# Decay steps of a gated linear attention scan moved and divided in a two-part transformer kernel

## The chip, the cores and the metric

The kernel runs on one core of one Trainium2 chip. The metric is the device time of one execution in microseconds (us), given as the median of several executions.

## What is computed

The reference is a stack of two blocks of two layers each, in fp32, on 256 tokens of width 1024. The change concerns the second block alone, which also carries 256 context tokens, so it works on 512 rows in layer 0 and, for most products, on 256 in layer 1. From the normalised rows h it makes, among others, keys and queries (4 heads of 128), values (4 heads of 256), two ranks of 16 for the decays, and the four inputs of a convolution branch. Its gated linear attention is:

```
la_f = log_sigmoid(r_f @ w_df + b_df) / 16      # and la_b for the backward scan
for each chunk (64 rows), state s (dk x dv per head):
    bcum  = cumsum(la)
    o     = (q * exp(bcum)) @ s  +  sum over s<=t of q k exp(bcum_t - bcum_s) v
    s_new = exp(b_last) * s + (k * exp(b_last - bcum))^T @ v
o_ctx, s_f, s_b = scans of the context (forward and backward), from zero
o_lat           = scans of the tokens, from s_f and s_b
```

In the last layer the context's outputs are not needed, only its end states. After the scan each head's rows are divided by their root mean square, and the result is gated, multiplied with a branch weight and summed with the two other branches.

## The kernel before, in words

**Weights.** Every weight is loaded by SyncE in units of 512 KB (`load`, L2812) into five RAW buffers, and split: ScalarE writes a high part in fp32r (`split`, L1523, its line in the profile L1529), VectorE the remainder (`split`, L2083, L2095). There are four pairs of split buffers (NS). A split into a buffer waits until TensorE has finished the unit that had it before. TensorE forms each product in three passes (high x high, low x high, high x low): `turned` (L1048 to L1050) for outputs with features along the partitions, `straight` (L1061 to L1063) for outputs with rows along them.

**Order of the work.** A class `Schedule` writes one list of steps, and each engine runs the steps of the list that concern it, strictly in the list's order. `get_w` appends the splits and loads that may go ahead; the split of unit u+3 stands in the list right ahead of the products of unit u. PSUM has eight banks; `take(ring, name)` gives the free bank of a ring that was let go longest ago, and `give` frees it in the list; at run time TensorE waits for the last reader of the bank's previous use (`bank`, L1014). LO4 are banks 0 to 3, HI4 4 to 7.

**The scan** (`gla`, L500 on) is a generator; each `next` appends some steps. The function `block2` calls it beside other work: once or more per unit of the values' products by the table KEYS, then beside the convolution branch (`branch_a`: 8 x 4 weight units, each appended as two halves) by `weave`. There each half unit adds RA (2.0 in layer 0, 1.25 in layer 1) to an account, and the scan goes on while the account is 1 or more; a `yield n` costs n, a plain `yield` 1. A scan handles the context (s = 1) first, then the tokens (s = 0). For each of them:

- `gdec` (TensorE L1269): eight products of the ranks RT with the decay weights WDEC into four banks. RT and WDEC are each made in a high part by ScalarE and a low part by VectorE in step `rank` (ScalarE L1710 and L1713, VectorE L2362 and L2366), after the raw decay weights WRAW have come by a DMA that ScalarE issues (`wdec`, L1705) behind the DMAs that store x (`spill2`, L1697).
- `gdec2` (VectorE L2380): 16 conversions of 128x256, eight taking the maximum with LOWEST into E4, eight the minimum into ET; ScalarE exponentiates E4 in two halves (L1745).
- `gln`: ScalarE takes two logarithms (L1752), VectorE combines them with ET (two of L2389), ScalarE exponentiates twice (L1757).
- `ginit`: the start values in GW; ScalarE copies the keys twice (L1766), VectorE multiplies the queries twice (L2405).
- the doubling: `gprod` (TensorE L1299, 16 products of 128 columns), `keep` (VectorE L2442, L2448) and `gwiden` (VectorE L2420, L2426, L2430; ScalarE L1778) over eight levels, IC apart in the account. Where the outputs aren't needed (layer 1, context), `gwiden` alone.
- for the context `gke` (keys turned, TensorE L1067, copied by ScalarE L1797), `gst` (end states, TensorE L1323, copied L1804).
- `gout` (outputs, L1339 to L1344, copied L1809), `gsq` (squares, ScalarE L1819), `gnorm` (VectorE's reciprocal root, then POOL L2752).

Before the change all of layer 0's scan lies beside the branch (KEYS is all 0), and layer 1's first decays, start values and widenings lie under the two groups of value units (`gv`, L1735 copies each group's four banks once its four units are done, L1738). The turned keys, the end states and layer 1's second decays lie beside the branch, whose first product is `ba_mm` (L1347). The convolution of the branch is `ba_x` (L1844, L2471 to L2479).

## Time and profile before

| what | value |
|---|---|
| median of 3 runs | 2110.48 us (2109.89 to 2114.09) |
| the profiled execution's own time | 2109.92 us |
| its span, first to last instruction | 2108.1 us |
| mean granted TensorE clock | 0.992 |
| TensorE busy | 2064.2 us, 98% |
| VectorE busy | 1355.6 us, 64% |
| ScalarE busy | 955.8 us, 45% |

The time of a run is that of the device, the span that of the profiled execution's instructions. Busy times count overlapping matmuls once, and a matmul's recorded length is longer than the distance to the next one. Times inside the trace count from the start of the span. The second block runs from about 690 us on, its layer 0 scan beside the branch from 788 to 1040, its layer 1 from about 1594, with the scan up to 1815.

### The profile page before, as it was taken

The numbers are of one execution on the slowest core, as the hardware profiler recorded it, in microseconds if no ns is written. First come the engines' busy times: TensorE is split into PE (matmuls) and PEld (weight loads), VectorE is DVE, ScalarE is ACT, GpSimd is POOL, SyncE is SP. The second block draws the span as 40 slices with busy tenths as digits, with TensorE's granted clock in tenths as the row PEclk, the third lists the DMA queues.
The fourth block names the chain that finished last, engine by engine and source line by source line (L and its number), as shares of the span: only waits on it lengthen the run. The fifth ranks groups of instructions, "written<-read, shape, count | busy, mean of one in ns | idle before, by whom it ended". The sixth has DMA issues, their size and how long they took to land.

```text
span 2108.1 us, 31387 instructions
## 1 busy us (share of the span) xinstructions
PE 2064.2 (98%) x12082; PEld 1781.1 (84%) x12082; DVE 1355.6 (64%) x2381; ACT 955.8 (45%) x1568; POOL 135.7 (6%) x140
## 2 busy tenths in 40 slices
PE   9999999999999999999999999999999989999998
PEld 6779998778999888888888778888888889888997
DVE  6757667667777328568445555868555588575665
ACT  5555555555555424353323453232244554445443
POOL 1001000000110100000200001111110000100100
PEclk9999999999999999999999999999999999999999
DMA  9437656525555422222222104534234334251553
GB/s 255 139 131 253 224 208 210 168 93 170 181 180 180 140 96 65 70 70 70 80 90 90 60 21 161 185 117 155 95 119 153 103 125 144 91 180 54 194 172 131
DMA packets 79731, 285.79 MB, mean 136 GB/s; under 512 B 8976, under 2 KB 9628, under 8 KB 79584
## 3 DMA queue, kind: packets, MB, share of 16 engines
q1 hardware_dynamic: 71136, 256.93, 36.4%
q10 hardware_dynamic: 6416, 19.51, 2.6%
q0 software_dynamic: 2032, 7.35, 1.4%
q8 instruction: 97, 1.59, 0.3%
q14 instruction: 50, 0.41, 0.1%
HBM read 277.92 MB, written 5.83 MB: 135 GB/s over the span
## 4 chain that ended last, share of the span: by engine, by line
PE 82%; DVE 9%; ACT 5%; issue 2%; POOL 0%; DVEq 0%; ACTq 0%
PE pb L1048 16%; PE pb L1050 16%; PE pb L1049 16%; PE pb L1061 6%; PE pb L1063 6%; PE pb L1062 6%; DVE SPL L2095 3%; PE pb L1067 2%; PE pb L1227 2%; PE pb L1228 2%; PE pb L1229 2%; PE pb L1299 2%; ACT SPH L1529 2%; PE pb L1402 2%; PE pb L1383 2%
## 5 line engine op out<-in xcount | busy, mean ns | idle before, releaser
L2095 DVE TENSOR_TENSOR SPL<-RAW,SPH 128x1024 fp32r<-128x1024 f32 x460 | 560.1, 1232 | 395.4 <-ACT SPH L1529 371.4
L1048 PE MATMUL pb<-HTH,SPH 128*128 128x256 f32 (+1 forms) x2008 | 645.9, 322 | 10.6 <-DVE SPL L2095 6.2
L1050 PE MATMUL pb<-HTH,SPL 128*128 128x256 f32 (+1 forms) x2008 | 637.8, 318 | 0.0
L1049 PE MATMUL pb<-HTL,SPH 128*128 128x256 f32 (+1 forms) x2008 | 637.6, 318 | 0.0
L1529 ACT ACTIVATE SPH<-RAW 128x1024 fp32r<-128x1024 f32 x462 | 478.3, 1051 | 238.9 <-PE pb L1050 117.7
L1048 PEld LDWEIGHTS pb<-HTH,SPH 128*128 128x128 f32 x2008 | 382.9, 191 | 39.5 <-issue 7.3
L1049 PEld LDWEIGHTS pb<-HTL,SPH 128*128 128x128 f32 x2008 | 383.0, 191 | 26.4
L1050 PEld LDWEIGHTS pb<-HTH,SPL 128*128 128x128 f32 x2008 | 382.7, 191 | 26.0
L1061 PE MATMUL pb<-SPH,HTH 128*128 128x512 f32 x640 | 255.0, 398 | 0.5 <-DVE QNB L2536 0.5
L1063 PE MATMUL pb<-SPL,HTH 128*128 128x512 f32 x640 | 250.3, 391 | 0.0
L1062 PE MATMUL pb<-SPH,HTL 128*128 128x512 f32 x640 | 250.3, 391 | 0.0
L1061 PEld LDWEIGHTS pb<-SPH,HTH 128*128 128x128 f32 x640 | 121.2, 189 | 27.2 <-issue 2.6
L1063 PEld LDWEIGHTS pb<-SPL,HTH 128*128 128x128 f32 x640 | 120.7, 189 | 26.0
L1062 PEld LDWEIGHTS pb<-SPH,HTL 128*128 128x128 f32 x640 | 121.0, 189 | 23.7
L1048 PE MATMUL pb<-ABH,SPH 128*128 128x512 f32 (+1 forms) x384 | 130.7, 340 | 1.7 <-DVE SPL L2095 0.9
L1049 PE MATMUL pb<-ABL,SPH 128*128 128x512 f32 (+1 forms) x384 | 128.9, 336 | 0.0
L1050 PE MATMUL pb<-ABH,SPL 128*128 128x512 f32 (+1 forms) x384 | 128.8, 335 | 0.0
L1896 ACT ACTIVATE GT<-pb,BG 128x512 f32<-128x512 f32 (+1 forms) x48 | 27.8, 579 | 118.5 <-PE pb L1050 118.5
L1048 PEld LDWEIGHTS pb<-ABH,SPH 128*128 128x128 f32 x384 | 72.1, 188 | 11.0 <-issue 2.2
L1050 PEld LDWEIGHTS pb<-ABH,SPL 128*128 128x128 f32 x384 | 72.0, 187 | 8.9
L1049 PEld LDWEIGHTS pb<-ABL,SPH 128*128 128x128 f32 x384 | 72.1, 188 | 8.6 <-issue 0.2
L1227 PE MATMUL pb<-SPH,AH 128*128 128x512 f32 x176 | 71.6, 407 | 2.2 <-ACT SPH L1529 1.8
(284 smaller groups left out, 2489.4 us busy)
## 6 DMA issues: line engine op xcount, KB each, us to landing
RAW<-in_w_up SPq DMA_DIRECT2D x88, 512.0 KB, 4.5
RAW<-in_wa SPq DMA_DIRECT2D x64, 512.0 KB, 3.3
RAW<-in_w_in SPq DMA_DIRECT2D x48, 512.0 KB, 5.1
RAW<-in_wmg SPq DMA_DIRECT2D x48, 512.0 KB, 3.3
RAW<-in_wbr SPq DMA_DIRECT2D x48, 512.0 KB, 3.3
RAW<-in_w_down SPq DMA_DIRECT2D x44, 512.0 KB, 4.7
RAW<-in_w_ada SPq DMA_DIRECT2D x24, 512.0 KB, 4.6
ARAW<-in_w_ada ACTq DMA_DIRECT2D x24, 512.0 KB, 4.3
```

The source lines that it names most:

```text
L1048: T.matmul(o, wh[:, kt, :], xh[:, kt, n0:n1], start=kt == 0, stop=False)
L1049: T.matmul(o, wh[:, kt, :], xl[:, kt, n0:n1], start=False, stop=False)
L1050: m = T.matmul(o, wl[:, kt, :], xh[:, kt, n0:n1], start=False, stop=kt == 7)
L1061: T.matmul(P[:, :], xh[:, kt, c], wh[:, j, :], start=kt == 0, stop=False)
L1062: T.matmul(P[:, :], xl[:, kt, c], wh[:, j, :], start=False, stop=False)
L1063: m = T.matmul(P[:, :], xh[:, kt, c], wl[:, j, :], start=False, stop=kt == 7)
L1067: return T.transpose(o, i, ident)
L1227: T.matmul(P[:, :], xh, wh, start=j == 0, stop=False)
L1228: T.matmul(P[:, :], xl, wh, start=False, stop=False)
L1229: m = T.matmul(P[:, :], xh, wl, start=False, stop=end)
L1529: A.activation(hi, raw, ACT.Copy, scale=1.0).then_inc(*act.tick(s["hi"], ("u", u)))
L2095: W.tensor_tensor(lo, raw, hi.bitcast(F32), SUB).then_inc(*dve.tick(s["lo_dve"], ("u", u)))
```

## The change

It divides the decays into three steps, `gdec2` (maximum conversions and first exponentials), `gln` (minimum conversions, logarithms, combination) and a new `gexp` (second exponentials), with other work between them by GAPS. E4 moves within the memory that GW, KE and XS share, so that it lies over two parts of GW that the turned keys KE don't use. The scan is written anew as a sequence: first decays, start values, doubling, keys turned, (layer 0: end states, outputs), second decays, (layer 1: end states), start values, (layer 0: norm of the first scan's rows), doubling, outputs, norm. In layer 0 the first decays and start values go under the second group of value units, which takes banks 4 to 7. In layer 1 one `next` of the scan follows each of the four key units, and KEYS gives 1, 2, 2, 2 and 2, 3, 1, 2 for the eight value units. IC, PC and the waits follow.

```diff
--- before.py
+++ after.py
@@ -33,8 +33,9 @@
 LO4, HI4, LOW6, LOW7, ALL8 = (0, 1, 2, 3), (4, 5, 6, 7), (0, 1, 2, 3, 4, 5), (0, 1, 2, 3, 4, 5, 6), (0, 1, 2, 3, 4, 5, 6, 7)
 
 RA = [2.0, 1.25]
-IC, PC = (4, 5), (8, 17)
-KEYS = ((0,) * 8, (2, 1, 1, 2, 2, 2, 2, 1))
+IC, PC = (4, 6), (3, 1)
+GAPS = ((1, 2), (2, 3))
+KEYS = ((0, 0, 0, 0, 1, 1, 1, 2), (1, 2, 2, 2, 2, 3, 1, 2))
 LOWEST = -30.0
 EARLY = 3
 FIRST = 11
@@ -555,66 +556,96 @@
             self.give(n)
             yield
 
+    def decays(self, l, s, ring):
+        self.add("mark", f"gla{l}{s}")
+        for i in range(4):
+            self.take(ring, ("gd", l, s, i))
+            self.add("gdec", l, s, i)
+        yield
+        self.add("gdec2", l, s)
+        yield GAPS[l][0]
+        self.add("gln", l, s)
+        for i in range(4):
+            self.give(("gd", l, s, i))
+        yield GAPS[l][1]
+        self.add("gexp", l, s)
+        yield
+
+    def doubling(self, l, s, ring):
+        full = gla_full(s, l)
+        if full:
+            for hp in range(2):
+                self.take(ring, ("gp", l, s, -1, hp))
+            self.add("gprod", l, s, -1)
+            yield LEAD[l][s]
+        for j in range(SPANS + full):
+            if full and j < SPANS:
+                for hp in range(2):
+                    self.take(ring, ("gp", l, s, j, hp))
+            if full:
+                self.add("keep", l, s, j - 1)
+                for hp in range(2):
+                    self.give(("gp", l, s, j - 1, hp))
+            if j < SPANS:
+                if full:
+                    self.add("gprod", l, s, j)
+                self.add("gwiden", l, s, j)
+            yield IC[l] if full else 1
+
+    def keys_turned(self, l, ring):
+        for i in range(4):
+            n = self.take(ring, ("ke", l, i))
+            self.add("gke", l, i)
+            self.give(n)
+            if i % 2:
+                yield
+
+    def states(self, l, ring):
+        for i in range(5):
+            if i < 4:
+                self.take(ring, ("st", l, i))
+                self.add("gst", l, i)
+            if i:
+                self.add("gst2", l, i - 1)
+                self.give(("st", l, i - 1))
+            yield
+
+    def outputs(self, l, s, ring):
+        for h in range(5):
+            if h < 4:
+                self.take(ring, ("go", l, s, h))
+                self.add("gout", l, s, h)
+            if h >= 1:
+                self.add("gout2", l, s, h - 1)
+                self.give(("go", l, s, h - 1))
+            yield
+
+    def rows_norm(self, l, s):
+        self.add("gsq", l, s)
+        yield
+        self.add("gnorm", l, s)
+        yield
+
     def gla(self, l, ring):
...
+        yield from self.decays(l, 1, ring if l else LO4)
+        self.add("ginit", l, 1)
+        yield
+        yield from self.doubling(l, 1, ring)
+        yield from self.keys_turned(l, ring)
+        if gla_full(1, l):
+            yield from self.states(l, ring)
+            yield from self.outputs(l, 1, ring)
+        yield from self.decays(l, 0, ring)
+        if not gla_full(1, l):
+            yield from self.states(l, ring)
+        yield PC[l]
+        self.add("ginit", l, 0)
+        yield
+        if gla_full(1, l):
+            yield from self.rows_norm(l, 1)
+        yield from self.doubling(l, 0, ring)
+        yield from self.outputs(l, 0, ring)
+        yield from self.rows_norm(l, 0)
 
     def branch_a(self, l, ring):
         for ft in range(8):
@@ -809,18 +840,20 @@
         self.add("rank", l, u, H)
         self.put_w(u)
         self.give(n)
+        scan, steps = self.gla(l, HI4), iter(KEYS[l])
         for ft in range(len(early), 4):
             u = self.get_w(f"wgk{l}", ft)
-            n = self.take(ALL8, ("gk", l, ft))
+            n = self.take(LO4 if last else ALL8, ("gk", l, ft))
             self.add("gk_mm", l, ft, u, None)
             self.put_w(u)
             self.add("gk", l, ft)
             self.give(n)
+            if last:
+                next(scan)
         if not last:
             drain(self.gla_queries(0, H))
-        scan, steps = self.gla(l, HI4), iter(KEYS[l])
         for g in range(2):
-            for _ in self.group_n(("gv", l, g), f"wgv{l}", g, (0, 1, 2, 3), LO4 if last else ALL8, H):
+            for _ in self.group_n(("gv", l, g), f"wgv{l}", g, (0, 1, 2, 3), HI4 if g and not last else LO4, H):
                 for _ in range(next(steps)):
                     next(scan)
             for t in range(4):
@@ -1740,17 +1773,19 @@
 
     def gdec2(l, st):
         for d in range(2):
-            e = sb["E4"][:, 2 * d:2 * d + 2, :].rearrange("p a n -> p (a n)")
+            e = sb["E4"][:, 3 * d, :]
             act.wait_ge(s["gla_dve"], ("z", l, st, d))
             A.activation(e, e, ACT.Exp, scale=-1.0).then_inc(*act.tick(s["gla_act"], ("ex", l, st, d)))
 
     def gln(l, st):
         for d in range(2):
-            e = sb["E4"][:, 2 * d:2 * d + 2, :].rearrange("p a n -> p (a n)")
+            e = sb["E4"][:, 3 * d, :]
             act.wait_ge(s["gla_act"], ("ex", l, st, d))
             act.wait_ge(s["const_dve"], "one")
             A.activation(e, e, ACT.Ln, scale=1.0, bias=sb["ONE"][:, 0:1]).then_inc(
                 *act.tick(s["gla_act"], ("ln", l, st, d)))
+
+    def gexp(l, st):
         for d in range(2):
             et = sb["ET"][:, d, :]
             act.wait_ge(s["gla_dve"], ("la", l, st, d))
@@ -1760,6 +1795,8 @@
         k.past(act, f"gla{l}{st}", SCAN)
         spilled(act, k, l)
         act.wait_ge(s["gla_dve"], ("la", l, st, 1))
+        if st == 0:
+            act.wait_ge(mm, ("st", l, 3))
         for ft in range(4):
             act.wait_ge(*k.read(("gk", l, ft)))
         for kind in (KF, KB):
@@ -1812,6 +1849,8 @@
 
     def gsq(l, st):
         k.past(act, f"gla{l}{st}")
+        if st == 0 and gla_full(1, l):
+            act.wait_ge(s["gla_dve"], ("gr", l, 1))
         for t in range(2):
             for h in range(4):
                 act.wait_ge(*k.read(("go", l, st, h)))
@@ -1977,7 +2016,7 @@
     does = {"start": start, "cs": cs, "lam": lam, "split": split, "ada_row": ada_row, "adv_load": adv_load, "stats": stats, "scale": scale,
             "prod": prod, "v_copy": v_copy, "qk_sums": qk_sums, "qk_turn": qk_turn, "scores": scores, "turn": turn1,
             "y": y, "y_turn": y_turn, "up": up, "tables": tables, "spill_ctx": spill_ctx, "spill_x": spill_x,
-            "spill2": spill2, "wdec": wdec, "rank": rank, "gk": gk, "gq": gq, "gv": gv, "gdec2": gdec2, "gln": gln,
+            "spill2": spill2, "wdec": wdec, "rank": rank, "gk": gk, "gq": gq, "gv": gv, "gdec2": gdec2, "gln": gln, "gexp": gexp,
             "ginit": ginit, "gwiden": gwiden,
             "keep": keep, "gke": gke, "gst2": gst2, "gout2": gout2, "gsq": gsq, "ba_c": ba_c, "ba_x": ba_x, "ba_z": ba_z, "split_a": split_a, "head_sum": head_sum,
             "head_turn": head_turn, "gate": gate, "scores2": scores2, "turn2": turn2, "values2": values2, "z": z,
@@ -2369,25 +2408,29 @@
     def gdec2(l, st):
         k.past(dve, f"gla{l}{st}", SCAN)
         spilled(dve, k, l)
-        for op, o in ((MAX, sb["E4"]), (MIN, sb["ET"][:, :, :].rearrange("p d (i n) -> p (d i) n", i=2))):
-            for i in range(4):
-                name = ("gd", l, st, i)
-                dve.wait_ge(mm, name)
-                for hh in range(2):
-                    c = slice(hh * 256, hh * 256 + 256)
-                    end = (dve.free(*k.read(name)) if op == MIN and hh else
-                           dve.tick(s["gla_dve"], *([("z", l, st, i // 2)] if op == MAX and hh and i % 2 else [])))
-                    W.tensor_scalar(o[:, i, c], k.P(name)[:, c], par("b_dec", l * 8 + i * 2 + hh), LOWEST, ADD,
-                                    op).then_inc(*end)
+        for i in range(4):
+            dve.wait_ge(mm, ("gd", l, st, i))
+            for hh in range(2):
+                c = slice(hh * 256, hh * 256 + 256)
+                W.tensor_scalar(sb["E4"][:, i // 2 * 3, i % 2 * 512 + hh * 256:i % 2 * 512 + hh * 256 + 256], k.P(("gd", l, st, i))[:, c], par("b_dec", l * 8 + i * 2 + hh),
+                                LOWEST, ADD, MAX).then_inc(
+                    *dve.tick(s["gla_dve"], *([("z", l, st, i // 2)] if hh and i % 2 else [])))
 
     def gln(l, st):
+        for i in range(4):
+            name = ("gd", l, st, i)
+            for hh in range(2):
+                c = slice(hh * 256, hh * 256 + 256)
+                W.tensor_scalar(sb["ET"][:, i // 2, i % 2 * 512 + hh * 256:i % 2 * 512 + hh * 256 + 256],
+                                k.P(name)[:, c], par("b_dec", l * 8 + i * 2 + hh), LOWEST, ADD, MIN).then_inc(
+                    *(dve.free(*k.read(name)) if hh else dve.tick(s["gla_dve"])))
         for d in range(2):
             et = sb["ET"][:, d, :]
             dve.wait_ge(s["gla_act"], ("ln", l, st, d))
             for i in (2 * d, 2 * d + 1):
                 dve.wait_ge(*k.read(("gd", l, st, i)))
             W.scalar_tensor_tensor(out=et, in0=et, scalar=-LOWEST,
-                                   in1=sb["E4"][:, 2 * d:2 * d + 2, :].rearrange("p a n -> p (a n)"), op0=ADD,
+                                   in1=sb["E4"][:, 3 * d, :], op0=ADD,
                                    op1=SUB).then_inc(*dve.tick(s["gla_dve"], ("la", l, st, d)))
 
     def ginit(l, st):
@@ -2396,6 +2439,8 @@
         for d in range(2):
             dve.wait_ge(s["gla_act"], ("et", l, st, d))
         dve.wait_ge(g, ("la", l, st, 1))
+        if st == 0:
+            dve.wait_ge(mm, ("st", l, 3))
         if not gla_full(st, l):
             return
         q = sb["GQ"][:, :, st * 256:(st + 1) * 256]
@@ -2452,6 +2497,8 @@
         GSS = sb["GSS"]
         for i in range(8):
             dve.wait_ge(s["gla_act"], ("gs", l, st, i))
+        if st == 0 and gla_full(1, l):
+            dve.wait_ge(s["gla_pool"], ("og", l, 3))
         rsqrt(s["gla_dve"], ("gr", l, st), GSS[:, 1, 0:8], GSS[:, 0, 0:8], 1.0 / 256, 8)
 
     def branch_tiles(l, ft):
@@ -2884,7 +2931,7 @@
     q = m.put("XS", C, [128, 4, 1024])
     m.put("QT", C, [128, 8, 512])
     m.put("ARAW", C, [128, 3, 1024])
-    m.put("E4", C + 8192, [128, 4, 512])
+    m.put("E4", C, [128, 4, 1024])
     m.put("GW", C, [128, 4, 1024])
     m.put("KE", C + 4096, [128, 4, 4, 128])
     m.put("KT", q, [128, 2, 512])
```

## Rows read from the trace of the kernel before

**Rows 1.** The page: busy time and share of the span, instructions per engine.

```profile
PE 2064.2 (98%) x12082; PEld 1781.1 (84%) x12082; DVE 1355.6 (64%) x2381; ACT 955.8 (45%) x1568; POOL 135.7 (6%) x140
```

**Rows 2.** Stretches: us; busy us (instructions) of each engine, granted clock, DMA share, GB/s.

```profile
940.00:960.00 20.00, 19.67 (x105) 16.70 (x104) 17.50 (x24) 7.32 (x8) 0.00 (x0) 1.00 0.17 63
960.00:1000.00 40.00, 39.63 (x214) 33.90 (x213) 32.73 (x46) 12.64 (x16) 0.00 (x0) 1.00 0.24 80
1600.00:1660.00 60.00, 60.00 (x270) 49.79 (x270) 37.06 (x47) 27.53 (x32) 0.00 (x0) 1.00 0.41 138
1740.00:1760.00 20.00, 19.73 (x168) 19.56 (x168) 18.84 (x29) 9.38 (x13) 0.00 (x0) 1.00 0.35 108
1760.00:1780.00 20.00, 19.15 (x163) 18.98 (x162) 18.39 (x29) 7.44 (x10) 0.00 (x0) 1.00 0.49 157
```

**Rows 3.** The same view, short stretches at two waits.

```profile
810.10:813.40 3.30, 3.30 (x17) 3.30 (x17) 3.20 (x4) 0.00 (x0) 0.00 (x0) 0.50 0.35 118
1697.50:1700.70 3.20, 0.00 (x0) 0.00 (x0) 1.30 (x2) 3.02 (x4) 0.00 (x0) 0.50 0.00 0
1700.90:1704.30 3.40, 3.40 (x16) 3.40 (x17) 2.75 (x5) 2.10 (x3) 0.00 (x0) 0.50 0.71 210
```

**Rows 4.** Timeline of layer 1's second decays: ScalarE, VectorE, TensorE. Start, length, line.

```profile
1690.48 1.06 ACT L1745 ACTIVATE E<-E 128x1024 f32<-128x1024 f32 x1 [0.51 <-DVE E L2380]
1691.56 1.28 ACT L1752 ACT_TABLE_LOAD   x1
1692.86 2.19 ACT L1752 ACTIVATE E<-E,ONE 128x1024 f32<-128x1024 f32 x2
1696.36 2.00 ACT L1757 ACTIVATE ET<-ET 128x1024 f32<-128x1024 f32 x2
1698.27 1.04 ACT L1529 ACTIVATE SPH<-RAW 128x1024 fp32r<-128x1024 f32 x1
...
1687.23 3.22 DVE L2380 TENSOR_SCALAR E<-pb,PAR 128x256 f32<-128x256 f32 x8
1694.04 2.36 DVE L2389 SCALAR_TENSOR_TENSOR ET<-ET,E 128x1024 f32<-128x1024 f32 x2 [0.46 <-ACT E L1752]
1699.39 2.44 DVE L2095 TENSOR_TENSOR SPL<-RAW,SPH 128x1024 fp32r<-128x1024 f32 x2 [2.99 <-issue]
...
1700.77 0.55 PE L1048 MATMUL pb<-HTH,SPH 128*128 128x256 f32 x1 [6.15 <-DVE SPL L2095]
```

**Rows 5.** Timeline of ScalarE at the last value unit of layer 1.

```profile
1659.56 1.06 ACT L1529 ACTIVATE SPH<-RAW 128x1024 fp32r<-128x1024 f32 x1 [4.38 <-PE pb L1063]
1660.86 0.60 ACT L1738 ACTIVATE GV<-pb 128x512 f32<-128x512 f32 x1 [0.24 <-PE pb L1063]
```

**Rows 6.** Timeline of TensorE: first products of the doubling, layer 0, both scans.

```profile
809.98 3.68 PE L1299 MATMUL pb<-GW,GK 128*128 128x128 f32 x16 [2.80 <-issue]
936.12 2.89 PE L1299 MATMUL pb<-GW,GK 128*128 128x128 f32 x16 [1.25 <-issue]
```

**Rows 7.** Timeline of VectorE and TensorE in layer 0's second scan.

```profile
955.44 1.35 DVE L2448 COPY_PREDICATED ATT<-MASK,pb 128x512 f32<-128x512 uint8 x2
...
959.43 0.79 PE L1299 MATMUL pb<-GW,KC 128*128 128x128 f32 x5 [0.33 <-DVE GW L2426]
```

**Rows 8.** Timeline at layer 1's ranks and first key unit: three engines.

```profile
1597.49 1.05 ACTq L1705 DMA_DIRECT2D WRAW<-in_wdec  x1
1605.89 1.06 ACT L1710 ACTIVATE WDEC<-WRAW 128x1024 fp32r<-128x1024 f32 x1 [6.25 <-DMA WRAW<-in_wdec]
...
1608.23 0.68 DVE L2366 TENSOR_TENSOR RT<-pb,RT 32x512 fp32r<-32x512 f32 x1
...
1598.45 0.40 PE L1048 MATMUL pb<-HTH,SPH 128*128 128x512 f32 x1
```

**Rows 9.** Timeline: a turned key's copy, and the second decays' products of layer 1.

```profile
1666.81 0.60 ACT L1797 ACTIVATE KE<-pb 128x512 f32<-128x512 f32 x1 [0.32 <-PE pb L1067]
...
1683.44 1.10 PE L1269 MATMUL pb<-RT,WDEC 128*128 128x256 f32 x8
```

59 lines of the change are left out of this document (removed).

## Prediction

> **What bounds the kernel now.** I read the page's busy shares first: TensorE is busy 98% of the span, VectorE 64%, ScalarE 45% [rows 1]. A change that only reorders steps can therefore win no more than TensorE's idle time and its time at the low clock. Two of its rows and the stretch table show where the two scans have any of it: in layer 0 2.80 us before 809.98 and 1.25 before 936.12 [rows 6], 0.33 and 0.37 in the stretches from 940 to 1000 [rows 2]; in layer 1 6.15 us before 1700.77 [rows 4] and 0.27 and 0.85 at 1740 to 1780 [rows 2]. In the stretch 1600 to 1660, where layer 1's keys and values are made, it is never idle. The short stretches show the clock: granted 0.50, which is 1.2 GHz, right behind the 2.80 us wait, and from 1697.5 to 1704.3 within and behind the long one [rows 3]; in the other stretches of the scans it is 1.00, 2.4 GHz [rows 2]. VectorE is nearly full in layer 1's second scan (18.84 and 18.39 of 20 us [rows 2]).
>
> The timeline names the cause. For layer 1's second decays VectorE starts at 1687.23 on twice eight conversions (eight take 3.22 us, the other eight as long), and ScalarE stays with exponentials and logarithms until 1698.36, neither with a weight split between [rows 4]. The next weight's high half comes at 1698.27, its low half at 1699.39; TensorE has eaten the stock by 1694.62 and sits idle 6.15 us. In layer 0 the same block makes the scan's start values late, and the first doubling products wait 2.80 us for them.
>
> **What is removed.** No instruction is added or taken away; steps move, and with them their place in every engine's queue. SyncE's loads keep their order, five ahead of the splits.
> (a) Layer 0's first decays go under the last value units, where a unit lasts 5.44 us (from split to split, 1.06 busy and 4.38 idle on ScalarE [rows 5]) and needs 1.05 us of ScalarE and 1.23 of VectorE. The 2.80 us wait goes. So does the low clock behind it: the sixteen products took 3.68 us there and 2.89 at full clock [rows 6], 0.8. Together 3.6.
> (b) Layer 0's second decays: split in steps, with the norm of the first scan's rows behind them. The start values are made four half units ahead of their first user, where it was two and a half. The wait of 1.25 us [rows 6] goes.
> (c) Layer 1's second decays leave the branch, whose products have 256 columns for 512 and so feed a weight through in about half the time. The 6.15 us wait goes, and the low clock from 1700.8 to 1704.3, half of 3.5, 1.75 [rows 3, 4]. Together 7.9.
> (d) Layer 1's second scan then has six units between levels for five, which is 4.8 half units for 4.0. VectorE's load in it falls with that, and I take the 0.27 and 0.85 at 1740 to 1780 as gone: 1.1.
> Sum of the gains 13.85 us.
>
> **What is added.**
> (e) The first scan of layer 0 falls on whole units, as the second does now. Where such a boundary is the x product, VectorE first does the convolution, masks only from 955.44, then widens, and TensorE waits 0.33 before 959.43 [rows 7]. Two of these per scan: 0.7. Bounds 0 and, if all eight boundaries had it, 2.6; I take the second scan's own count.
> (f) **Layer 1's first decays are now queued on TensorE directly behind the first key unit.** That unit starts at 1598.45 and lasts 5.44, so it is done at 1603.9. The decay products need the decay weights' low part and the ranks' low part. Their raw load was issued at 1597.49 behind two stores of 1 MB each on ScalarE's queue; ScalarE gets it at 1605.89 after 6.25 us of waiting, and VectorE writes the last part from 1608.23 to 1608.91 [rows 8]. None of this moves. Today four more units stand between and cover it. So TensorE stands still from 1603.9 to 1609.0, 5.1 us, with three key units queued behind it. That is the cover that is gone.
> (g) **Layer 1's second decays end in front of the copies that empty the values' banks.** The keys give 4 nexts, then 1, 2, 2, 2, 2, 3, 1, 2. Counting: decays 4 nexts, start 1, eight widenings, keys turned 2, decays 4, sum 19, all used. So the logarithm and exponential steps are put after the last value unit but before `gv`'s four copies on ScalarE. The branch's first product takes one of the banks 0 to 3, all four held by the values (the other four hold the decays), so it waits for the first copy. Clock from the end of the sixth value unit: four turned keys copied, 2.7; weight split 1.05 to 3.75 and 1.23 to 5.1; eight conversions 3.2 to 8.3; second exponential to 9.4; split 1.05 to 10.4 and 1.23 to 11.7; eight conversions 3.2 to 14.9; two combinations 2.36 to 17.2; last exponential 1.06 to 18.3; copy 0.60 to 18.85 [rows 4, 5, 9]. The table loads of 1.28 lie mostly beside VectorE's work. TensorE: the turnings, and eight decay products of 1.10 together, the last bank free at 2.7, to 3.05, two units to 13.95. It waits 4.9 us. Below, 3 us if VectorE starts its second eight before the split; above, the 6.15 of today's block.
> (h) The clock behind (f) and (g). Today's rows bound it: 2.80 us of idling was followed by a low stretch of 3.4, of which the products felt 0.8; 6.15 us by one that cost 1.75 outside the wait. I take 1.2 for each, 2.4; bounds 0 and 3.4 for each (a low stretch of 6.8 wholly behind the wait).
> (i) The decay products wait for the turned keys' copies: 0.2.
> Sum of the losses 0.7 + 5.1 + 4.9 + 2.4 + 0.2 = 13.3. Net 0.55 us faster.
>
> In ScalarE's rows the activation behind a table load starts 0.02 us after the load's end (1691.56 + 1.28, next at 1692.86 [rows 4]), so a switch costs 1.3 us here. The Trainium skill, "ScalarE: Activation LUTs", section "What ACT_TABLE_LOAD costs", counts a drain of 1380 ns on top, 2.66 us a switch. By that page each of the two switches of (g) would be longer by 1.38 us, an estimate of up to 2.8 us more wait. The trace does not agree, and the sum leaves it out.
>
> **The sum against the times.** The profiled execution took 2109.92 us around a span of 2108.1, 1.8 us outside it, which nothing here touches; 2109.92 - 0.55 = 2109.4. The median of the three runs is 2110.48, 0.56 above it, so I forecast a median of 2109.9. A measurement of this kernel can tell about 0.2%, 4.2 us.
>
> **The rivals.**
> 1. **One of the two new waits does not come** (the raw decay weights land earlier; or the chain of (g) is paced by ScalarE alone and reaches the copies in time). For it: in 1600 to 1660 VectorE has 22.9 us free and ScalarE 32.5 [rows 2], and the stores that hold up the raw decay weights may land sooner in another run. Against it: both follow from order in queues, not from load. Then 5.1 + 1.2 or 4.9 + 1.2 are not lost: 2103.7. If neither comes, 2097.5. Chance 0.25 for the two.
> 2. **Slower: a third wait at layer 0's seam between values and branch.** There the branch has banks 0 to 3 free at once, but its first doubling product needs two of banks 4 to 7, emptied by copies that now stand behind the exponentials and the start values' two copies (128x1024, some 1.05 us each as the passes of [rows 4]). From the start of the last value unit I get: split, load, two exponentials, two start copies to 6.4, two bank copies to 7.5; TensorE arrives at 5.44 + 2.72 = 8.2. It decides when the second copy ends more than 0.7 us later than I have it. If that chain were paced as late as layer 1's in (g), whose first copy starts 9.7 us into the last unit, plus 2.0 for the start copies and 1.1 for two bank copies, it ends at 12.8: wait 4.6 and 1.2 of clock, 2115.7. Against it: here VectorE's second eight start a whole unit earlier. Chance 0.14.
> 3. **Each switch of tables takes a second load's time again.** The chain of (g) has two switches and would grow by 2 x 1.28 = 2.6 us [rows 4]: 2112.5, if ScalarE and not VectorE paces it there. Against it stands the gap of 0.02 us behind the load. Chance 0.03, within 0.2% too. The Trainium skill's drain ("ScalarE: Activation LUTs", "What ACT_TABLE_LOAD costs") is such a rule, and by its figure the time would be an estimate of 2112.7.
>
> **How the numbers follow.** Forecast as summed 0.58, its own range 2106.5 to 2113.5: (g) from 3 to 6.15, (h) from 0 to 3.4 twice, seldom at the same end. Within 0.2% (2106.3 to 2114.7): 0.58 + 0.03, less 0.01 for ends = 0.60. Faster 0.25, slower 0.15. The range reaches down to rival 1's single case, 2103.0, and up to 2114.5; beyond it lie rival 2 and the case of neither wait.
>
> **What would show it.** Right: no wait over 1 us on TensorE at 800 to 1000; the split-bound wait at 1694 gone; instead about 5 us of idle ahead of the first decay products of layer 1, ended by VectorE's write of the ranks, and about 5 us ahead of the branch's first product in layer 1, ended by ScalarE's copy of the values; low clock behind each. Wrong: if either wait is under 2 us, the time is nearer 2104; if the doubling products of layer 0 wait for value copies, rival 2 holds.

## The result and the profile after

The changed kernel takes 2118.43 us (median of 6, 2116.77 to 2120.71), the kernel before 2110.18 (median of 6, 2109.52 to 2114.09): 1.0038 of it, 95% interval 1.0028 to 1.0048. It is slower by 8.2 us. The forecast was 2109.9, no change, with a range from 2103.0 to 2114.5. The profiled execution took 2118.12 us around a span of 2116.3.

The page's busy line answers to [rows 1]: every engine does the same work, and TensorE is busy 4.7 us longer in a span that is 8.2 longer. So this is waiting and low clock (a product at half clock is busy for longer), not work.

```profile
PE 2068.9 (98%) x12082; PEld 1784.3 (84%) x12082; DVE 1361.3 (64%) x2381; ACT 954.2 (45%) x1568; POOL 134.9 (6%) x140
```

Where the 8.2 us arise is read from steps that both kernels make in the same place. The view by tile, kernel before: first and last start of a group stand behind its durations.

```profile
L1710 ACT ACTIVATE WDEC<-WRAW x2: 1050/1055/1060, 712.5 to 1605.9; 128x1024 fp32r<-128x1024 f32 x2
L1049 PE MATMUL pb<-ABL,SPH x384: 276/340/398, 1059.5 to 2078.7; 128*128 128x512 f32 x96, 128*128 128x256 f32 x96
L1857 ACT ACTIVATE ABH<-AF x16: 399/515/637, 1037.3 to 1824.8; 128x512 fp32r<-128x512 f32 x8, 128x256 fp32r<-128x256 f32 x8
```

The same three groups in the changed kernel, and the first product of layer 1's first key unit, which starts at 1598.45 in the kernel before [rows 8].

```profile
L1743 ACT ACTIVATE WDEC<-WRAW x2: 1053/1054/1056, 713.6 to 1608.9; 128x1024 fp32r<-128x1024 f32 x2
L1082 PE MATMUL pb<-ABL,SPH x384: 276/338/398, 1062.1 to 2086.9; 128*128 128x512 f32 x96, 128*128 128x256 f32 x96
L1896 ACT ACTIVATE ABH<-AF x16: 399/516/633, 1037.0 to 1833.0; 128x512 fp32r<-128x512 f32 x8, 128x256 fp32r<-128x256 f32 x8
...
1601.92 0.39 PE L1081 MATMUL pb<-HTH,SPH 128*128 128x512 f32 x1
```

Layer 0's decay weights are 1.1 us late, before a moved instruction has run. Layer 0's scans end 2.6 late (1059.5, 1062.1): they cost 1.5, where the forecast has a gain of 4.15 ((a), (b) less (e)). Layer 1's first key unit is 3.5 late. The step behind its scans is 8.2 late (1824.8, 1833.0): 4.7 more, where the forecast has 3.6. From there to the end nothing changes (2078.7, 2086.9). The 0.9 between the scans is not of the change's making: no step moved there, and the twelve executions differ by 2.1 in this stretch (the table behind experiment 10).

The view of the waits names what TensorE idles for, here from 1590 to 1800.

```profile
PE pb L1302 <- DVE RT L2405: 4.5, 1, 4.5
PE pb L1081 <- ACT GV L1771: 4.3, 1, 4.3
PE pb L1149 <- DVE DG L2211: 3.7, 1, 3.7
PE pb L1332 <- DVE GW L2471: 0.2, 1, 0.2
```

The first two are the new waits (f) and (g). The third lies at the seam of the two layers, ahead of the scans, where no step moved; the kernel before waits 1.2 us there and 2.9 at 1571. The 6.15 us ended by a weight split [rows 4] is gone, and of the two waits at 1740 to 1780 0.2 is left.

**Loss (f).** The timeline of the changed kernel at layer 1's ranks (start, length, engine, line), which answers to [rows 8]:

```profile
1608.87 1.06 ACT L1743 ACTIVATE WDEC<-WRAW 128x1024 fp32r<-128x1024 f32 x1 [6.27 <-DMA WRAW<-in_wdec]
1611.21 0.68 DVE L2405 TENSOR_TENSOR RT<-pb,RT 32x512 fp32r<-32x512 f32 x1
1611.99 2.01 PE L1302 MATMUL pb<-RT,WDEC 128*128 128x256 f32 x8 [4.48 <-DVE RT L2405]
```

**Loss (g).** The timeline at the end of layer 1's values, which answers to [rows 4, 5]:

```profile
1673.75 1.28 ACT L1785 ACT_TABLE_LOAD   x1
1675.05 2.19 ACT L1785 ACTIVATE E<-E,ONE 128x1024 f32<-128x1024 f32 x2
1677.26 1.28 ACT L1792 ACT_TABLE_LOAD   x1
1679.35 2.19 ACT L1792 ACTIVATE ET<-ET 128x1024 f32<-128x1024 f32 x2 [0.81 <-DVE ET L2432]
1681.45 2.04 ACT L1771 ACTIVATE GV<-pb 128x512 f32<-128x512 f32 x4
...
1682.08 0.58 PE L1081 MATMUL pb<-HTH,SPH 128*128 128x256 f32 x1 [4.31 <-ACT GV L1771]
```

Both are as the forecast wrote them: ranks' low part into the first decay products, logarithms and exponentials ahead of the copies, the first copy frees the branch's bank. The activation behind a table load again starts 0.02 us after its end (1673.75 + 1.28, 1675.05), so rival 3's second load is not there.

**What was not forecast** stands in layer 0's second decays. The timeline there, GpSimd first, then VectorE, then TensorE:

```profile
919.68 4.20 POOL L2799 TENSOR_TENSOR GV<-GV,GSS 128x1024 f32<-128x1024 f32 x2 [215.62 <-DVE GSS L2072]
...
917.82 0.17 DVE L2051 TENSOR_SCALAR RS<-GSS 128x8 f32<-128x8 f32 x1 [2.13 <-ACT SQ L1858]
...
919.52 0.68 DVE L2542 SCALAR_TENSOR_TENSOR WA<-WA,pb 128x512 f32<-128x512 f32 x1
920.24 1.89 DVE L2547 TENSOR_TENSOR AF<-WA 128x512 f32<-128x512 f32 x1
922.05 2.91 DVE L2134 TENSOR_TENSOR SPL<-RAW,SPH 128x1024 fp32r<-128x1024 f32 x1
924.88 1.28 DVE L2487 SCALAR_TENSOR_TENSOR ATT<-pb,IDENT 128x512 f32<-128x512 f32 x2
...
928.77 3.28 PE L1332 MATMUL pb<-GW,KC 128*128 128x128 f32 x16 [3.12 <-DVE GW L2471]
...
938.48 2.02 PE L1332 MATMUL pb<-GW,KC 128*128 128x128 f32 x16 [0.56 <-DVE GW L2471]
```

The split of line 2134 takes 2.91 us for its usual 1.23, the product of line 2547 1.89 for 0.69: 2.9 us of VectorE, just ahead of the widened keys of the doubling. TensorE waits 3.12 us for them and then runs at the low clock. GpSimd's two multiplications, the norm of the first scan's rows, lie under exactly these two. Ahead of them the norm holds VectorE in another way: it stands still 2.13 us, until ScalarE has made the last of the eight squares, and then does the nine small steps of the reciprocal root (917.82 to 919.61). In the kernel before the multiplications lay under something else (timelines of the kernel before, GpSimd and VectorE):

```profile
914.16 4.69 POOL L2752 TENSOR_TENSOR GV<-GV,GSS 128x1024 f32<-128x1024 f32 x2 [209.70 <-DVE GSS L2033]
...
914.02 1.23 DVE L2095 TENSOR_TENSOR SPL<-RAW,SPH 128x1024 fp32r<-128x1024 f32 x1
915.16 3.22 DVE L2380 TENSOR_SCALAR E<-pb,PAR 128x256 f32<-128x256 f32 x8
918.30 3.21 DVE L2380 TENSOR_SCALAR ET<-pb,PAR 128x256 f32<-128x256 f32 x8
```

The conversions out of the banks keep their usual 3.22 per eight, and the split that began 0.14 us ahead of GpSimd its 1.23.

**The clock.** Stretches of the changed kernel with their granted clock, in the columns of [rows 2]:

```profile
704.10:707.50 3.40, 3.29 (x15) 3.32 (x16) 1.49 (x2) 1.78 (x3) 0.00 (x0) 0.50 0.98 351
929.40:932.80 3.40, 3.40 (x16) 3.21 (x15) 2.61 (x4) 0.90 (x2) 0.00 (x0) 0.50 0.18 46
1612.00:1615.40 3.40, 3.40 (x12) 3.11 (x13) 3.37 (x5) 0.79 (x1) 0.00 (x0) 0.51 0.36 31
1682.20:1687.10 4.90, 4.90 (x18) 4.45 (x19) 1.23 (x1) 2.23 (x4) 0.00 (x0) 0.50 0.08 18
```

Behind each of the three long waits 3.4 to 4.9 us of work run at half clock: 1.7, 1.7 and 2.45. The first stretch lies ahead of every moved step; four of the twelve profiles of this study have it and eight, that of before among them, do not, so it belongs to the execution and not to the change. So does the 1.1 us at 713.6: the same step starts between 709.8 and 715.6 in the twelve profiles, and at 713.6 to 714.3 in three that have no low clock there.

### The profile page after: what moved, and what is told of

It reads as the page before. It is cut to its first block and busy times, and to the rows that moved or that the text cites. A ratio compares the mean times of both kernels' runs of the same rounds, so it can differ in the third digit from the quotient of the medians.

```text
span 2116.3 us, 31382 instructions
## 1 busy us (share of the span) xinstructions
PE 2068.9 (98%) x12082; PEld 1784.3 (84%) x12082; DVE 1361.3 (64%) x2381; ACT 954.2 (45%) x1568; POOL 134.9 (6%) x140
```

## The experiments

The kernel before was timed again beside each group of runs: 2110.87 for experiments 1 to 4, 2110.81 for 5 to 8, 2111.47 for 9 and 10, which ran on another chip. Ratios are to it. Where an edit is shown in part, `...` marks what is left out.

**1. The norm back ahead of the second decays.**

```
             yield from self.outputs(l, 1, ring)
+            yield from self.rows_norm(l, 1)
...
         self.add("ginit", l, 0)
         yield
-        if gla_full(1, l):
-            yield from self.rows_norm(l, 1)
```

> Edit: the norm of the first scan's rows in layer 0 goes back ahead of the second decays, where the kernel before had it; all else as changed (2118.4 us). Theory A (GpSimd's two multiplications of that norm slow VectorE while they run: in the changed kernel a product of the convolution took 1.88 us for 0.69 and a split 2.91 for 1.23 beside them, and the next doubling products waited 3.1 us, with low clock behind): beside the second decays' conversions, which read PSUM, they slow nothing, the wait goes, and with it 3.3 + 1.6 us: 2113.5, the wait before the second doubling products under 0.7 us. Theory B (the wait comes from VectorE's own added work, the nine passes of the reciprocal root, 1.8 us, and its place ahead of the start values now delays those): the wait only moves to the start values, as the 1.25 us of the kernel before, 2116 to 2118.

Measured 2121.08, 1.0049 (1.0037 to 1.0061): slower still, which neither theory had. Timeline of this run: GpSimd, VectorE, TensorE.

```profile
903.95 3.93 POOL L2798 TENSOR_TENSOR GV<-GV,GSS 128x1024 f32<-128x1024 f32 x2 [197.88 <-DVE GSS L2071]
...
905.26 0.86 DVE L2522 SCALAR_TENSOR_TENSOR WA<-WA,PAR 128x255 f32<-128x255 f32 x1 [0.79 <-ACT WA L1882]
906.15 2.00 DVE L2525 SCALAR_TENSOR_TENSOR WA<-WA,PAR 128x255 f32<-128x255 f32 x1
...
925.96 3.75 PE L1331 MATMUL pb<-GW,GK 128*128 128x128 f32 x16 [5.13 <-DVE GW L2449]
```

Here the multiplications fall on the convolution's passes (0.48 us each elsewhere), which stand ahead of the conversions. They hold VectorE up by 1.9 us (0.86 and 2.00 for 0.48 each). All of the decays is late, and TensorE waits 1.7 and 5.13 us. Most of that is order: the norm's two steps put the decays later in the list, behind the convolution, so that their conversions begin 12.4 us after the decay products (896.83, 909.23), where it is 3.5 us in the changed kernel (892.06, 895.52). So the experiment shows what else the norm's place moves, and does not decide between the theories.

**2. GpSimd's multiplication cut to one column of 256 for these rows.**

```
-            v = V(sb["GV"][:, st * 2 + t, 0:1], [256, 4], [1, 256])
-            G.tensor_tensor(v, v, V(sb["GSS"][:, 1, t * 4:t * 4 + 1], [1, 4], [0, 256]), MUL).then_inc(
+            n = 1 if st else 256
+            v = V(sb["GV"][:, st * 2 + t, 0:1], [256, 4], [1, n])
+            G.tensor_tensor(v, v, V(sb["GSS"][:, 1, t * 4:t * 4 + 1], [1, 4], [0, n]), MUL).then_inc(
```

> Edit: the changed kernel with the two multiplications of the context rows' norm on GpSimd cut to one column of 256 (it leaves out nearly all of that scaling, in both places in layer 0 alone where s = 1). Nothing else moves, VectorE's nine passes stay where they are. Theory A (the slowing comes from GpSimd running beside VectorE): the product of the convolution is back at 0.69 us and the split at 1.23, the wait of 3.1 us before the second doubling products falls under 0.5, about 2113.5. Theory B (VectorE's own work): the wait stays above 2 us and the time within 1 us of 2118.4.

Measured 2115.8, 1.0028 (1.0017 to 1.0038): 2.6 less than the changed kernel, where theory A had 4.9. VectorE and TensorE in this run:

```profile
919.46 0.69 DVE L2547 TENSOR_TENSOR AF<-WA 128x512 f32<-128x512 f32 x1
920.07 1.22 DVE L2134 TENSOR_TENSOR SPL<-RAW,SPH 128x1024 fp32r<-128x1024 f32 x1
...
925.12 2.16 PE L1332 MATMUL pb<-GW,KC 128*128 128x128 f32 x16 [0.23 <-ACT KC L1815]
934.80 2.02 PE L1332 MATMUL pb<-GW,KC 128*128 128x128 f32 x16 [2.09 <-DVE GW L2471]
```

With the multiplications all but gone both passes have their usual length and the 3.12 us wait is 0.23: the cause of that wait is shown. A second wait of 2.09 then shows one level later, where the changed kernel has 0.56 (938.48). The low clock hides it there: TensorE is slow, and VectorE catches up. Experiment 3, whose layer 0 is that of the changed kernel, shows this without any edit: in its execution the clock stays up behind the wait of 3.12 us, and the second wait is there in full.

```profile
934.70 2.02 PE L1337 MATMUL pb<-GW,KC 128*128 128x128 f32 x16 [2.09 <-DVE GW L2476]
```

Experiment 5 is the same (3.12, full clock, 2.10); experiments 4 and 7 have the low clock and a second wait of 0.54 and 0.57.

**3. Layer 1's value copies ahead of the logarithm and exponential steps.**

```
-            for _ in self.group_n(("gv", l, g), f"wgv{l}", g, (0, 1, 2, 3), HI4 if g and not last else LO4, H):
+            for i, _ in enumerate(self.group_n(("gv", l, g), f"wgv{l}", g, (0, 1, 2, 3),
+                                               HI4 if g and not last else LO4, H)):
+                if i == 3 and last:
+                    for t in range(4):
+                        self.add("gv", l, g, t)
+                        self.give(("gv", l, g, t))
                 for _ in range(next(steps)):
                     next(scan)
-            for t in range(4):
+            for t in range(0 if last else 4):
...
```

> Edit: in layer 1 the four copies that empty the last values' banks are queued ahead of the logarithm and exponential steps of the second decays; nothing else. Theory A (the branch's first product waited 4.3 us for the first of those copies, which stood behind ScalarE's chain): the wait goes and the low clock behind it, 4.5 + 2.4 us, so about 2111.5; the chain itself runs on beside the first branch units, whose splits are three units ahead, without a wait over 1 us. Theory B (the chain is as long and now holds up the weight splits beside the short branch units, as in the kernel before): a wait of 3 to 6 us comes back some 10 us later, 2116 to 2119.

Measured 2111.78, 1.0003 (0.9995 to 1.0012), 6.6 less than the changed kernel. TensorE's waits from 1590 to 1800:

```profile
PE pb L1307 <- DVE RT L2410: 4.5, 1, 4.5
PE pb L1337 <- DVE GW L2476: 0.2, 1, 0.2
```

The wait of (g) is gone with its low clock, 4.31 + 2.45 = 6.8 in the changed kernel's trace, and nothing takes its place. It was a matter of order alone.

**4. The decay weights' load ahead of the two stores.**

```
-        self.add("wdec", l)
+        if not last:
+            self.add("wdec", l)
...
+            self.add("wdec", 1)
             self.add("spill2")
```

> Edit: layer 1's load of the raw decay weights is issued just ahead of the two stores of x on ScalarE's queue in place of behind them. Theory A (the first decay products of layer 1 waited 4.5 us because this load lay behind 2 MB of stores): it lands in about 4.5 us after its issue instead of 8.4, ScalarE's idle time before the high parts falls from 6.3 to about 2 us or less, the ranks' low part is written some 4 us sooner, the wait falls to about 0.5 us and the low clock behind it goes: 2118.4 - 5.8 = 2112.6. Theory B (the load shares the same DMA engines with the stores wherever it stands in the queue, and lands as late): the wait stays over 3 us, 2117 to 2119.

Measured 2120.6, 1.0046 (1.0034 to 1.0058): a miss for both theories. ScalarE's and TensorE's rows:

```profile
1611.08 1.06 ACT L1745 ACTIVATE WDEC<-WRAW 128x1024 fp32r<-128x1024 f32 x1 [8.54 <-DMA xscr<-XS]
...
1614.20 2.04 PE L1304 MATMUL pb<-RT,WDEC 128*128 128x256 f32 x8 [6.71 <-DVE RT L2407]
```

By the view of the transfers the load now lands 4.1 us after its issue (8.4 in the changed kernel), yet ScalarE waits for the stores. The code says why: the `rank` step waits first for the phase mark `proj1`, and a mark stands for the last signal that its engine has raised. That was the load; with the order turned it is the second store. So the edit put a longer wait in the place of the one it removed, and says nothing against (f).

**5. Layer 1's first decays behind the second key unit.**

```
-            if last:
+            if last and ft:
                 next(scan)
-KEYS = ((0, 0, 0, 0, 1, 1, 1, 2), (1, 2, 2, 2, 2, 3, 1, 2))
+KEYS = ((0, 0, 0, 0, 1, 1, 1, 2), (2, 2, 2, 2, 2, 3, 1, 2))
```

> Edit: in layer 1 the first decays' four products stand behind the second key unit and no longer behind the first; the first value unit takes one step of the scan more, so that everything from there on stands where it was. Theory A, loss (f) of the prediction: TensorE's 4.5 us idle ahead of the decay products and the low clock behind it (1.85 us) are there only because one key unit of 5.4 us is too little cover for the late decay weights; with a second unit the cover is complete, both go, and the time is 2118.4 - 6.3 = 2112.1, 1.0009 of before. Theory B: the chain behind the products (conversions, exponential, split steps) is then a unit late, and the wait comes back ahead of the first doubling products of layer 1 or in its keys' turning: at least half the gain is lost, 2115.3 or more.

Measured 2112.08, 1.0006 (0.9997 to 1.0016), against 2112.1 expected. The eight products of 256 columns run without idle before them, at full clock (2.01 in the changed kernel):

```profile
1614.44 1.11 PE L1302 MATMUL pb<-RT,WDEC 128*128 128x256 f32 x8
```

One unit more of cover is all that (f) lacked in this execution; experiment 8 has one in which it isn't quite enough.

**6. The norm behind layer 0's whole second doubling, nothing left out.**

```
-        if gla_full(1, l):
-            yield from self.rows_norm(l, 1)
         yield from self.doubling(l, 0, ring)
+        if gla_full(1, l):
+            yield from self.rows_norm(l, 1)
```

> Edit: layer 0's norm of the first scan's rows stands behind the whole second doubling, not between the second decays' start values and the doubling; nothing is left out. Theory A, the cause shown by cutting GpSimd's multiplications to one column: what hurts is GpSimd's two passes of 4.2 us beside VectorE's SBUF-to-SBUF passes right ahead of the start values, and not the norm as such. Moved to a place where VectorE's backlog is short, the 3.1 us wait near 925 falls to under 0.6 and its low clock goes, 4.7; as in that run the wait at the convolution's boundary near 932 then shows, up to 1.5 more than now: 2115.2, 1.0024 of before, between 2114 and 2117. Theory B: the passes cost VectorE their 2.9 us wherever they lie, and the wait turns up again behind the second doubling, ahead of the output products or of layer 0's branch: 2118 or more.

Measured 2112.36, 1.0006 (0.9997 to 1.0015): 6.1 less than the changed kernel, where 3.2 was expected, and below theory A's 2114. TensorE's waits from 780 to 1010:

```profile
PE pb L1332 <- DVE GW L2471: 0.5, 2, 0.3
PE pb L1302 <- ACT GV L1846: 0.5, 1, 0.5
```

Not only the 3.12 us wait is gone; the 2.09 that experiment 2 laid bare is too. The rest of the norm, eight squares on ScalarE (913.26 to 917.69 in the changed kernel) and nine small steps on VectorE ahead of the same keys, is therefore a cost of that place as well. In experiment 2 VectorE stands still 2.14 us for the last square and is then busy 1.8 with the small steps, 3.9 us that it doesn't lose at this place now. Which of the two makes the 2.09 was not taken apart. The multiplications now lie at 984.23 (4.66 us), where VectorE has an idle stretch of 9.4.

**7 and 8. The mendings together.** Experiment 7 has the edits of 3 and 5, experiment 8 those of 3, 5 and 6.

> Edit: layer 1's two mendings together: the values' bank copies ahead of the logarithm and exponential steps (measured alone: 6.6 us less than the changed kernel) and the first decays behind the second key unit. Theory A, the two waits are independent of each other: 2118.4 - 6.6 - 6.3 = 2105.5, 0.9978 of before. Theory B: they share VectorE's and ScalarE's backlog, so that with the decays a unit later the copies or the start values are late again in the branch, and a wait of 2 us or more with low clock behind it is seen between 1675 and 1700: 2108.5 or more.

> Edit: the two mendings of layer 1 and the norm behind the second doubling in layer 0. Theory A, the three faults of the changed kernel are independent: 2118.4 - 6.6 - 6.3 - 3.2 = 2102.3, 0.9963 of before, faster than both kernels; waits over 1 us are left only near 932, at 1580 and at the branches' ordinary places. Theory B: one of the three comes back elsewhere: 2105 or more.

Measured 2105.49, 0.9978 (0.9969 to 0.9987), and 2098.02, 0.9945 (0.9932 to 0.9958). The second beats both kernels: 12.8 us less than before, and 4.3 less than theory A had. The gains add up about: 6.65 + 6.35 + 6.07 = 19.1 singly, 20.4 together by medians. Part of that is the executions' own: from 713 us on the profile of experiment 8 is 18.1 shorter than that of the changed kernel, and 11.0 shorter than that of before. In experiment 8 TensorE's waits from 1595 to 1800 are

```profile
PE pb L1307 <- DVE RT L2410: 1.4, 1, 1.4
PE pb L1337 <- DVE GW L2476: 0.2, 1, 0.2
```

and between 500 and 2090 the granted clock never falls. Of (f) 1.4 us is back in this execution, because the load of the decay weights landed later, 10.2 us after its issue (8.9 in experiment 5); experiments 5 and 7 have none of it.

**9. The best version with layer 1's levels 5 apart in the account, as before the change, and not 6.** At 1.25 to a half unit that is 4.0 half units of the branch for 4.8.

```
-IC, PC = (4, 6), (3, 1)
+IC, PC = (4, 5), (3, 1)
```

> Edit: the version with all three mendings, and layer 1's doubling levels five branch units apart, as they were before the change, and not six. Theory A, gain (d) of the prediction: six units give VectorE 4.8 half units a level for 4.0, and with five its load between 1700 and 1780 is back near the 18.8 and 18.4 of 20 us of the kernel before, with idle of about 1.1 us on TensorE there: 2098.0 + 1.1 = 2099.1. Theory B: with the second decays out of the branch VectorE has no backlog when the levels begin, and the spacing makes no difference: 2098.0 within 0.5, and no wait over 0.4 us between 1700 and 1780. Five rounds tell some 2 us, so the profile has to decide between the two.

Measured 2104.27, 0.9965 (0.9953 to 0.9977): 4.8 more than experiment 10, which was timed beside it on the same chip, and 6 more than experiment 8, against 1.1 expected. The waits from 1595 to 1800:

```profile
PE pb L1337 <- DVE GW L2476: 3.2, 4, 1.4
PE pb L1086 <- DVE SPL L2139: 0.5, 1, 0.5
```

Two stretches of the same run, in the columns of [rows 2]:

```profile
1700.00:1720.00 20.00, 19.18 (x163) 19.00 (x163) 17.79 (x26) 8.98 (x12) 0.00 (x0) 1.00 0.34 106
1720.00:1740.00 20.00, 18.10 (x153) 17.75 (x152) 17.57 (x25) 9.09 (x12) 0.00 (x0) 1.00 0.35 109
```

Theory A has the sign and the releaser right (the keys that VectorE widens) and both sizes wrong. With 5 the boundaries wait 3.2 us and a weight split 0.5, 3.7 in all, where the kernel before lost 1.1 and experiment 8 loses 0.2. So the sixth is worth 3.5 here: without it, moving the second decays out of the branch would have given nearly half of its 7.9 back. VectorE is not fuller for it: 17.8 and 17.6 of 20 us, and 17.5 and 18.3 in the same stretches of experiment 8. The widening comes too late at each boundary, but a lack of room on VectorE isn't shown. Of the 5.8 us between the profiles of experiments 9 and 10, 3.8 lie in layer 1's scans, 1.3 at the seam of the layers, where the clock is low from 1583.3 to 1590.1 in experiment 9 alone, and 0.7 ahead of 713 us.

**10. The best version with layer 1's first decays behind the third key unit.**

```
-KEYS = ((0, 0, 0, 0, 1, 1, 1, 2), (2, 2, 2, 2, 2, 3, 1, 2))
+KEYS = ((0, 0, 0, 0, 1, 1, 1, 2), (3, 2, 2, 2, 2, 3, 1, 2))
...
-            if last and ft:
+            if last and ft > 1:
```

> Edit: the version with all three mendings, with layer 1's first decays behind the third key unit and not the second; the first value unit takes the step more. In the profile of that version the decay weights' load landed late enough for 1.4 us of idle ahead of the decay products, which in the two earlier runs with the second unit was not there. Theory A: a third unit of 5.4 us covers the load wherever it lands, up to 1.4 us less: 2096.6 to 2098.0, and no wait ahead of the decay products. Theory B: the chain behind them is now too late for layer 1's first widened keys and their turning, or for the second decays, with a wait of over 1 us between 1630 and 1690: 2099 or more.

Measured 2099.49, 0.9944 (0.9932 to 0.9956). The 1.4 us wait is gone, and no wait over 0.4 is seen from 1630 to 1800; the time is that of experiment 8 within the intervals, and 1.5 above theory A's upper end. Behind the third unit the load was covered in this execution; behind the second it was in experiments 5, 7 and 9 and was not in 8.

**The stretches of the profiles side by side.** "Layer 0" runs from the first high part of the decay weights to the first product with ABL, which stands behind the scans; "seam" from there to layer 1's first key unit; "layer 1" from that to the last step ABH<-AF, behind its scans. From there to the end all twelve take 253.9 to 254.1. "Low" is whether the clock was low behind the 3.12 us wait ahead of the widened keys, where the profile has that wait.

| profile | layer 0 | low | seam | layer 1 |
|---|---|---|---|---|
| before | 347.0 | | 539.0 | 226.4 |
| changed kernel | 348.5 | yes | 539.8 | 231.1 |
| 1, norm ahead | 351.7 | | 540.5 | 231.8 |
| 4, load first | 348.6 | yes | 539.3 | 234.5 |
| 3, copies first | 348.6 | no | 541.0 | 224.1 |
| 5, decays a unit later | 348.6 | no | 541.1 | 224.4 |
| 7, both of these | 348.6 | yes | 539.2 | 217.9 |
| 2, one column | 345.7 | | 540.8 | 230.3 |
| 6, norm behind the doubling | 342.7 | | 540.5 | 233.5 |
| 8, all three | 342.8 | | 539.0 | 219.5 |
| 9, levels 5 apart | 342.8 | | 540.4 | 222.0 |
| 10, third key unit | 342.8 | | 539.1 | 218.2 |

Layer 0 is the same within 0.1 us wherever its steps are the same, whether the clock fell or not. In layer 1 the wait for the decay weights' load varies between executions (3.4 to 5.4 us where the decays stand behind the first key unit, and 6.7 in experiment 4).

## Why the prediction was wrong

**The step that failed is (b).** It said that with the norm of the first scan's rows put behind them, layer 0's second decays are only earlier, and the wait of 1.25 us goes. It costed the norm's new place at nothing and named none of the queues that the norm is moved in, GpSimd's among them. The start values are early, as forecast, and the 1.25 us wait is gone. But the next link, the first widened keys, waits 3.12 us, against the prediction's own sign of being right, no wait over 1 us at 800 to 1000. Behind it the low clock takes 1.7, or, where the clock stays up, a second wait of 2.09 comes. The norm at this place costs 5.8 us: layer 0 takes 348.5 or 348.6 with it and 342.7 or 342.8 without it (experiments 6, 8, 9 and 10). GpSimd's multiplications are 2.9 of that (experiment 2), and what is left of the norm, the squares and the small steps, the other 2.9. With this term the sum would have been 2115.7. The prediction looked at the start values, not at what is late next.

**(a) and (c) right.** Neither the 2.80 us at layer 0's seam nor the 6.15 of layer 1 [rows 4, 6] is in the trace of after. With the norm out of the way layer 0 gains 4.2 us on the kernel before (347.0, 342.8), where (a), (b) and (e) together have 4.15.

**(d) right in size for the kernel before** (1.1 gone but 0.2), for too small a reason: experiment 9 shows that the sixth step of spacing is worth 3.5 us once the decays have left the branch.

**(e)** 0.7 said; the first doubling's two boundaries wait 0.5 together. Another 0.5 was not thought of: the second scan's decay products wait for a bank that the first scan's output copy holds (the second line of the waits of experiment 6, the same in the changed kernel).

**(f) and (g) right in place, releaser and almost in size:** 4.48 for 5.1 and 4.31 for 4.9. **(h) was too small:** 1.7 and 2.45 behind them for 2.4 together. (f), (g) and (h) come to 12.9 for 12.4, and to 13.2 by what experiment 7 takes out of layer 1. The rows of before had bounded the clock's part between 0 and 3.4 for each wait; 1.2 each was taken, near the 0.8 us felt behind the 2.80 us wait. In this execution each of the three waits over 3 us has 1.7 us or more behind it; it is no rule, for in experiments 3 and 5 the clock stays up behind the same 3.12 us wait.

In sum, layer 1's scans cost 4.7 for 3.6: 0.8 is (f), (g) and (h), 13.2 for 12.4, and 0.3 is (c) and (d) less (i), 8.5 (226.4, 217.9) for 8.8. Layer 0 costs 1.5 for a gain of 4.15: that is the norm. Another 2.0, ahead of the first moved step and between the scans, is the executions' own. With the norm moved alone (experiment 6) the kernel takes 2112.4, 2.5 above the forecast. **Rival 2** had the right sign with the wrong place: no doubling product of layer 0's first scan waits for the value copies. Rival 1 did not come true; rival 3 did not either.

## What to carry to other kernels

Work that is moved out of one engine's way still occupies the others that execute it: list its instructions by engine, and for GpSimd's look at what VectorE does in the same microseconds, because two engines can stand in each other's way without a semaphore between them. When a step moves ahead of others in a queue, ask of each place whether what it needs can be there (f) and whose banks stay full behind it (g); both waits were read off the order before the run, and each was mended by moving one step of the list. Gains of separate stages add up where the stages share no backlog, and the spacing of a loop has to be looked at again once something has left it.

## What was not expected of the hardware

**VectorE stands still beside GpSimd, for some passes and not others.** With GpSimd's two multiplications at 919.68 to 923.88, 2.10 us each, the product with two SBUF inputs that began at 920.24 ended at 922.13, 0.35 after the first multiplication; the split that began at 922.05 ended at 924.96, 1.08 after the second, and 1.23 is its own length. Experiment 1 shows the same: the convolution pass that began at 906.15 ended at 908.15, 0.27 after GpSimd. Conversions from PSUM with one input kept 0.40 us each beside it, and splits that began 0.14 us (before) ahead of GpSimd kept their length, 1.23; there GpSimd's two took 4.69 (4.66 in experiment 6, behind a split begun 0.16 us ahead) for the 4.20 of the changed kernel. Each of the held passes ends within its own length after the end of a multiplication, whenever it began. That fits a pass held up until GpSimd is done, and not two engines at half speed. The Trainium skill, "SBUF — State Buffer", section "Who interferes with whom", says that a VectorE instruction with two SBUF inputs contends with a GpSimd instruction that reads SBUF, that the port pair which they share is an exclusive lock, and that the order of issue decides who blocks. By that rule, the traces agree in all of these cases.

**A low clock can hide a wait, and here it cost nothing by itself.** In the changed kernel TensorE ran at 0.50 from 929.4 to 932.8 behind its wait of 3.12 us, which gave VectorE time, and the next wait was 0.56. In experiments 3 and 5 the same steps had the same 3.12, the clock stayed at 1.00, and the next wait was 2.09 and 2.10. Layer 0 took 348.5 or 348.6 us either way. Removing the first wait alone is therefore worth 2.9 by the traces (2.6 by medians) and not 3.12 + 1.7, until the second is removed as well.
